# Two late experts instead of three, gathers from SyncE's queue, and output in column halves, in a hybrid encoder layer with a mixture of experts

## The reference

```python
hid = silu(einsum('td,edf->tef', hf, w1[gi])) * einsum('td,edf->tef', hf, w3[gi])
out = out + einsum('tef,efd->td', hid * combine[:, gi, :, None], w2[gi])
...
x = x + gt2 * hier_moe(h, ...)
return rms_norm(x, final_norm_g)
```

## Time and profile before

| | |
|---|---|
| median of 3 runs | 692.84 us (692.42 to 694.58) |
| profiled execution | 693.55 us |
| its span, first to last instruction | 691.7 us |
| TensorE, VectorE, ScalarE, GpSimd busy | 96%, 61%, 38%, 10% |
| moved by DMA | 201.25 MB, mean 291 GB/s |

### The profile page before, as it was taken

One profiled execution on the slowest core, in us unless ns is written; L12 is line 12 of the kernel. 1 busy time (PEld: TensorE's weight loads), 2 busy tenths in 40 slices (PEclk: granted clock), 3 DMA queues, 4 the chain that ended last, 5 costly groups with the idle time before them and its releaser, 6 DMA issues.

```text
span 691.7 us, 12844 instructions
## 1 busy us (share of the span) xinstructions
PE 666.5 (96%) x5402; PEld 535.8 (77%) x5402; DVE 419.8 (61%) x710; ACT 264.5 (38%) x373; POOL 71.4 (10%) x70
## 2 busy tenths in 40 slices
PE   8999999999999999999999998999999999999893
PEld 7999999998777777999989997675666666665441
DVE  4656888987866789977787788644232122121226
ACT  3346554657763624336552343221132121221102
POOL 0001000000003614300000000001111111111111
PEclk9999999999999999999999999999999999999997
DMA  8997774455343443346639996999999999999992
GB/s 361 422 367 260 284 263 168 134 179 189 121 153 139 145 161 123 122 132 259 232 101 406 422 385 251 422 403 416 410 377 422 419 422 421 418 418 418 420 381 91
DMA packets 31196, 201.25 MB, mean 291 GB/s; under 512 B 5047, under 2 KB 5431, under 8 KB 7970
## 3 DMA queue, kind: packets, MB, share of 16 engines
q1 hardware_dynamic: 27378, 193.27, 71.7%
q0 software_dynamic: 3760, 7.14, 2.8%
HBM read 195.35 MB, written 10.75 MB: 298 GB/s over the span
## 4 chain that ended last, share of the span: by engine, by line
PE 74%; DMA 10%; DVE 8%; ACT 3%; issue 2%; SPq 1%; DVEq 0%; POOLq 0%; ACTq 0%
PE ps L1571 72%; DMA ring<-in_pieces 4%; DMA ring<-in_expert_pieces 4%; DVE ring_rounded L934 3%; ACT ring_rounded L644 2%; SPq L461 1%; PE ps L1715 1%; DMA r_z<-y_rows 1%; DMA y_rows<-r_st,r_btm 1%; PE ps L2011 1%; DVE r_ct L1209 1%; DVE r_v L1209 1%; DVE x_sb L1522 1%; DVE r_kq L1173 0%; DVE r_xs_rounded L1239 0%
## 5 line engine op out<-in xcount | busy, mean ns | idle before, releaser
L934 DVE TENSOR_TENSOR ring_rounded<-ring,ring_rounded 128x2048 fp32r<-128x2048 f32 x60 | 136.6, 2289 | 34.0 <-ACT ring_rounded L644 33.6
L1571 PE MATMUL ps<-hT_rounded,ring_rounded 128*128 128x256 f32 x832 | 148.7, 285 | 0.7 <-ACT hT_rounded L658 0.7
L1571 PEld LDWEIGHTS ps<-hT_rounded,ring_rounded 128*128 128x128 f32 x832 | 127.9, 191 | 4.6 <-issue 3.5
L644 ACT CAST ring_rounded<-ring 128x2048 fp32r<-128x2048 f32 x60 | 114.0, 1906 | 28.3 <-DMA ring<-in_pieces 20.0
L1571 PE MATMUL ps<-ring_rounded,hT_rounded 128*128 128x512 f32 x352 | 112.4, 396 | 0.0
L1571 PE MATMUL ps<-x_sb_rounded,ring_rounded 128*128 128x256 f32 x416 | 94.9, 283 | 0.0
L1571 PEld LDWEIGHTS ps<-x_sb_rounded,ring_rounded 128*128 128x128 f32 x416 | 76.4, 191 | 0.9 <-issue 0.2
L1571 PEld LDWEIGHTS ps<-ring_rounded,hT_rounded 128*128 128x128 f32 x352 | 65.9, 190 | 14.4 <-issue 1.7
L858 ACT ACTIVATE sq<-ps 128x128 f32<-128x128 f32 x32 | 8.9, 277 | 141.7 <-PE ps L1571 141.7
L1454 DVE TENSOR_TENSOR r_st<-ps,r_kq 128x512 f32<-128x512 f32 x32 | 22.1, 691 | 64.9 <-PE ps L1571 64.8
L603 POOL DMA_INDIRECT y_rows<-r_st,r_btm x29 | 28.5, 984 | 306.8 <-DVE r_st L1454 300.7
(11 more groups left out here) (336 smaller groups left out, 998.4 us busy)
## 6 DMA issues: line engine op xcount, KB each, us to landing
ring<-in_pieces SPq DMA_DIRECT2D x66, 1024.0 KB, 5.2
ring<-in_expert_pieces SPq DMA_DIRECT2D x48, 1024.0 KB, 17.0
r_z<-in_expert_pieces SPq DMA_DIRECT2D x12, 1024.0 KB, 12.6
r_xs<-in_expert_pieces SPq DMA_DIRECT2D x12, 1024.0 KB, 12.3
r_v<-in_pieces SPq DMA_DIRECT2D x6, 1024.0 KB, 7.8
r_ct<-in_pieces SPq DMA_DIRECT2D x6, 1024.0 KB, 5.5
g_sb<-in_expert_pieces SPq DMA_DIRECT2D x6, 1024.0 KB, 17.0
r_st<-in_expert_pieces SPq DMA_DIRECT2D x6, 1024.0 KB, 17.6
```

The source lines that it names most:

```text
L644: nc.scalar.copy(high_of(p_), slot_of(p_)).then_inc(hi_ok, 1)
L934: nc.vector.tensor_tensor(low_of(p_), slot_of(p_), high_of(p_).bitcast(F32), ALU.subtract).then_inc(lo_ok, 1)
L1571: return nc.tensor.matmul(o, l, r, start=start, stop=stop)
```

## The change

`LATE` goes from 3 to 2, so expert 29 is scattered through memory like the 29 before it. The four gathers are issued by SyncE, behind its weights, and no longer by GpSimd. The last scaling and the stores of both tiles are done in two halves of 512 columns. The two copies of the transposed picks become one. The diff, cut to its core:

```diff
-LATE = 3
+LATE = 2
...
@@ sync
             for k in range(4):
                 sp.wait_ge(y_stored[k], 16 * len(range(k, EARLY_E, 4)))
+            rows_of_tokens = y_rows.rearrange("(n k) d -> n (k d)", k=4)
+            for t in range(TT):
+                for c_ in range(2):
+                    sp.dma_start(y_two[:, t, c_], rows_of_tokens[t * P:(t + 1) * P, c_ * D:(c_ + 1) * D]
+                                 ).then_inc(y_two_ok[2 * t + c_], 16)
...
-            sp.wait_ge(fin_done, 1)
-            sp.dma_start(out[0, 0:P, :], x_sb[:, 0]).then_inc(out_done, 16)
-            sp.wait_ge(out_ready, 1)
-            sp.dma_start(out[0, P:2 * P, :], x_sb[:, 1]).then_inc(out_done, 16)
-            sp.wait_ge(out_done, 16 * TT)
+            for h in range(2):
+                cs = slice(h * CW, (h + 1) * CW)
+                sp.wait_ge(fin_done, h + 1)
+                sp.dma_start(out[0, 0:P, cs], x_sb[:, 0, cs]).then_inc(out_done, 16)
+                sp.wait_ge(out_ready, h + 1)
+                sp.dma_start(out[0, P:2 * P, cs], x_sb[:, 1, cs]).then_inc(out_done, 16)
+            sp.wait_ge(out_done, 16 * 2 * TT)
@@ gpsimd
-            for k in range(4):
-                pool.wait_ge(y_stored[k], 16 * len(range(k, EARLY_E, 4)))
-            rows_of_tokens = y_rows.rearrange("(n k) d -> n (k d)", k=4)
-            for t in range(TT):
-                for c_ in range(2):
-                    pool.dma_start(y_two[:, t, c_], rows_of_tokens[t * P:(t + 1) * P, c_ * D:(c_ + 1) * D]
-                                   ).then_inc(y_two_ok[2 * t + c_], 16)
@@ scalar
-            nc.scalar.mul(x_sb[:, 0], x_scaled, st[:, 8:9]).then_inc(fin_done, 1)
+            for h in range(2):
+                cs = slice(h * CW, (h + 1) * CW)
+                nc.scalar.mul(x_sb[:, 0, cs], x_scaled[:, cs], st[:, 8:9]).then_inc(fin_done, 1)
@@ vector
-                nc.vector.tensor_copy(flat[:, 0:512], ps[4][:])
-                nc.vector.tensor_copy(flat[:, 512:], ps[5][:, 0:(LATE * TT - 4) * P]).then_inc(late_back, 1)
+                nc.vector.tensor_copy(flat, ps[4][:, 0:LATE * TT * P]).then_inc(late_back, 1)
...
-            hidden_turned(EARLY_E)
+            hidden_turned(E - 2)
             rows_of_late_experts()
-            output(EARLY_E)
-            hidden(EARLY_E + 1)
-            hidden_turned(EARLY_E + 1)
-            output(EARLY_E + 1)
+            output(E - 2)
             hidden(E - 1)
             hidden_turned(E - 1)
             add_gathered(0, 0)
             add_gathered(0, 1)
...
-            nc.vector.scalar_tensor_tensor(x_sb[:, 1], x_sb[:, 1], st[:, 9:10], fng, ALU.mult, ALU.mult).then_inc(out_ready, 1)
+            for h in range(2):
+                cs = slice(h * CW, (h + 1) * CW)
+                nc.vector.scalar_tensor_tensor(x_sb[:, 1, cs], x_sb[:, 1, cs], st[:, 9:10], fng[:, cs], ALU.mult, ALU.mult
+                                               ).then_inc(out_ready, 1)
@@ tensor
-            turn_of(EARLY_E)
+            turn_of(E - 2)
             late_rows_turned()
-            down_of(EARLY_E)
-            up_of(E - 2)
-            scatter(EARLY_E, 0)
-            turn_of(E - 2)
-            scatter(EARLY_E, 1)
             down_of(E - 2)
             up_of(E - 1)
             scatter(E - 2, 0)
```

More of the change, by code:

```diff
@@ L2067, in late_rows_turned @@
                         n_t = i * TT + t
-                        ins = nc.tensor.transpose(ps[4 + n_t // 4][:, n_t % 4 * P:(n_t % 4 + 1) * P],
+                        ins = nc.tensor.transpose(ps[4][:, n_t * P:(n_t + 1) * P],
                                                   late_pick[:, i, t].rearrange("p h r -> p (h r)"), ident)
```

## The result

The change is slower: 697.16 us median of 12 runs (695.28 to 700.5) against 694.20 for the kernel before on the same chip (12 runs, 692.42 to 694.85), so the medians are 3.0 us apart. The ratio on record is taken over all the runs and is not that of the two medians: 1.0057, with a 95% interval of 1.0042 to 1.0073. The forecast, +3.3, lies between the two. Two slow executions, of 950 and 1112 us at 0.65 and 0.56 of TensorE's full clock, are left out of all ratios.

What follows compares the result with a forecast made beforehand. Late bound: two transfers in a row, expert 28's store and the first gather, with TensorE's path 0.22 us apart. 693.55 + 3.7 - 0.4 = 696.85; from the median, 692.84 + 3.3 = 696.1 us; range 693.4 to 699.2.

Steps and rivals of the forecast that it cites:

- The forecast case: Last stretch: expert 29's store and the gather behind it delay output 31; +3.3 us, 696.1, own range 695.0 to 698.0; chance 0.63.
- Part 1: TensorE does up(30) before down(29): its second half starts at 663.81, output 29 at 668.43, store issued 669.95, landing 676.15.
- Weights of up(30) that land away from 663.8: TensorE's late stretch: sign of a wrong forecast, which left the landing of these weights where it was.
- The store at its lowest price: GpSimd's store of expert 29's rows: lands 6.2 us after issue, the lowest on record, since weights are nearly all in.
- three microseconds before anything moves: Store of expert 29's rows: three microseconds pass before its packets move, and lighter traffic needn't shorten them.
- The gather's price: First gather behind expert 29's store: 2.7 us, from the 512 KB output store, landing at 678.95; other end 7.5.
- SyncE's queue: Gathers moved from GpSimd to SyncE: the change of queue credited with nothing more; the shorter gather comes from the emptier time.
- Halves: Last scaling and output stores in halves: first quarter issued some 0.5 us earlier, -0.4 us, bounds 0.55 gain or 0.
- The rival in which TensorE's path decides: Before output 31: gathers come in time and TensorE's path sets the end; +0.7 us, 693.5; chance 0.15.
- the removed scatters buy nothing: TensorE's late path: two scatter steps taken away, 1.13 us each, gain nothing, replaced by an exposed wait for weights.
- The clock's rival: TensorE's wait for output 31: the clock falls, a scatter takes 2.3 us, adds wait 1.1 more; 697.2; chance 0.10.
- Small parts at nothing: Turn(27)'s four extra one-column matmuls and VectorE's tiny index operation: cost 0, covered by TensorE's 0.52 us weight wait.

Runs made afterwards that it cites:

- LATE = 2 alone: Kernel before with two late experts in the change's TensorE order, but gathers still on GpSimd and whole tiles at the end; ratio 1.0049.
- gathers that read the input: The change, with its four gathers reading input x in place of y_rows behind the same waits, early experts' sum left out; ratio 1.0020.
- down(29) first: The change, but TensorE does turn(29) and down(29) ahead of up(30), as before; expert 29 still stored and gathered; ratio 1.0010.
- clock kept: The change with 14 filler products in place of 3 while TensorE waits for output 31; ratio 1.0042.

## Why the prediction was right

The forecast case happened, for its reason: one more store behind down(29), with a gather behind it. Against a forecast of +3.3 us the times say +4.0 (+3.0 by the medians), and the median of 697.16 us is well inside the range. That the number came so close is partly luck, as the sum below shows. Point by point:

- **Part 1, the order of TensorE: right in its steps, wrong in where it starts.** From up(30)'s second half to output 29 it is 4.61 us (I had 4.62), and to the store's issue 6.14 (6.14). But I had left that half's weights where they landed before, 6.4 us behind the start of down(28) (194.0 since the first store). In all eight executions with two late experts they are in 5.0 to 5.1 us behind it (192.6 in the change's). With three it is 6.1 to 6.6 in four executions and 5.0 in the fifth. "Weights of up(30) that land away from 663.8" was one of my signs of being wrong, and it came. Why they come sooner no run shows.
- **The store at its lowest price: right.** 6.08 us against 6.2, and 5.2 to 6.1 in the four other executions with that store and order. That it is no queue behind weights holds: the weights' share of the engines was 45% in the first microsecond and 3% in the last two. But my picture of it, three microseconds before anything moves, fell: with the weights thinning out, most of the 80 packets moved in the second microsecond, and the landing came as late as ever. What the later microseconds go to, beside a few late packets, no row shows. The formula of the Trainium skill ("DMA: Bandwidth & Descriptors", anatomy of one DMA on the GpSimd path) would have given an estimated 2.6 us; no run agrees with it for this indirect store, the least being 5.2.
- **The gather's price: the term that was mis-sized.** I took 2.7 us, from a store of the same size. Measured were 4.29 us in the change and 4.45, 4.0 and 4.0 in three executions beside it: +1.6. Part of it may be the company of the three gathers behind it, which I had given no price and which no run takes away. The second row then came 1.74 us behind the first, not 1.28, so the second add waited 0.53, of which I had none.
- **The sum over these steps.** Since the first store, output 31 begins at 212.66 in the change where I had 681.66 - 469.81 = 211.85, 0.8 later. That is -1.4 from the weights, -0.1 from the store, +0.3 from SyncE (0.39 us from landing to issue, where I had 0.1), +1.6 from the gather and +0.4 from the second row. So misses of opposite sign hid each other, by luck. The span's end is at 226.3 against a forecast of 221.9 + 3.3 = 225.2; the times put the miss at 0.7 us (interval -0.4 to +1.8).
- **SyncE's queue: right, worth nothing.** With the weights gone 4.29 us against GpSimd's 4.45; beside weights 7.8 against 7.5; and a ratio of 1.0002 for this part by itself. The rule of the Trainium skill, "DMA: Bandwidth & Descriptors", under the rules for kernel authors, that another issuing engine saves only sequencer time, agrees with these.
- **Halves: right in kind, half the size.** I took -0.4. The rows give -0.24 and -0.28; the times can't tell it from nothing.
- **The rival in which TensorE's path decides** was priced at +0.7 us. Without expert 29's store the times say +0.1 (-1.3 to +1.4), which neither shows nor excludes it. But the delay of down(31) under it, 677.09 - 675.80 = 1.3 us by my working, is under 0.2 when counted from down(28), since the weights of up(30) were in 1.3 us sooner than I had them. That the removed scatters buy nothing holds.
- **The clock's rival took place as well**, and I gave it 0.10. I had priced it at 1.1 us on the path. What it costs depends on when it falls. In the change's profile that is 0.7 us into the last scatters, which then take 3.09 us, but their first pair only 1.40: between output 31 and the end of the sums it is 6.04 us against 5.79 before. With LATE = 2 alone, and with gathers that read the input, it had fallen before the scatters began; their first pair took 2.10 and the same stretch 6.74 and 6.73, so 0.95 on the path. The run that keeps the clock is not told apart in time. So it was no rival to the forecast case but a part of it, 0.25 to 0.95 us by these rows.
- **Small parts at nothing: right.** The run without expert 29's store has all of them and loses nothing that the times tell. Down(28), which stands behind turn(27)'s extra matmuls, starts 188.1 us after the first store in the mean of the eight executions with two late experts, and 188.0 in the mean of the five with three.

What stays open: what the clock costs on average, which the times don't resolve; why the weights of up(30) land sooner with two late experts; and how the gather's price is divided between y_rows, reading as such and the three gathers beside it.

## What to carry to other kernels

Work that is moved from late on a compute engine to a store and a gather through memory must be issued early enough for the two in a row, here 5.2 to 6.1 plus 4.0 to 4.5 us even with the weights nearly gone; count back from where the rows are wanted before moving it. When only the order within that part was wrong, the order alone gives most of it back (1.0057 to 1.0010 by doing down(29) first). And before putting one step of a waiting engine ahead of others, look at which of the two things it waits for lands first: VectorE's adds ahead of output 31 are right while rows land before down(31) ends, and swapping them cost 0.4%.

## What the runs showed of the hardware

- The first of four reads of 512 KB from memory, with the weights gone, took 4.0 to 4.5 us to land (3.6 from the input), the first of two stores of 512 KB to memory 2.7. I had taken the two for equal.
- An indirect store of rows took 5.2 us at the least, with the weights thinning out, 7.55 in one case among them and behind another store, and up to 10.2 before.
- Four matmul records of 64 rows each (64x512, one scatter) take 1.13 us, eight (two scatters) 1.99, and four of 128 rows (128x512, the diagonal product) 1.98. So two 64-row products cost about as much as one of 128 rows, and appear to run beside each other. That is an inference from these three durations; no run tests it.
- TensorE's clock fell to 1.2 GHz while it stood idle, 3.7 us after its last matmul before the change and 3.7 with LATE = 2 alone (last matmul to 679.59, mean clock 0.66 over 683 to 684). In the change it fell only when TensorE, 4.46 us idle, had been at work again for 0.7 us. It stayed at 2.4 GHz through the last scatters behind waits of 0.69 us (clock kept) and 0.92 (down(29) first).
